# Compression stage of a hybrid decoder step: turned rows written in the order place, group, block

## The reference, cut to what matters

```python
def compress(kr, pe, w1, w2, nb):
    b, _, g, d = kr.shape                       # d = 128
    blk = kr[:, :nb * CMP_BLOCK].reshape(b, nb, CMP_BLOCK, g, d) + pe[None, None, :, None, :]
    blk = jnp.transpose(blk, (0, 1, 3, 2, 4)).reshape(b, nb, g, CMP_BLOCK * d)
    return jax.nn.silu(blk @ w1) @ w2           # w1: 4096 x 256, w2: 256 x 128
```

## Time and profile before

| | |
|---|---|
| median of 3 runs | 3240.89 us (3238.18 to 3242.6) |
| span of the profiled execution | 3241.6 us |
| PE busy | 2938.7 us, 91% of the span |
| PEld, DVE, ACT, POOL busy | 2604.9, 1365.9, 711.1, 131.9 us |
| line 1041, keys, MATMUL x512 | 118.2 us busy, 393 ns each |
| line 1041, values, MATMUL x512 | 117.2 us busy, 390 ns each |
| compress stage, keys | about 1155 to 1352 us of the span |
| compress stage, values | about 1352 to 1555 us of the span |
| granted clock over the span | 0.943 |

### The profile page before, as it was taken

How to read it: one execution, slowest core, us unless ns; L and a number is a source line. 1 busy time by engine, 2 the same in 40 slices (tenths; PEclk the granted TensorE clock), 3 DMA queues, 4 the chain that set the end, 5 groups by cost and what they waited for, 6 DMA issues and landing times. The chain is left out here.

```text
span 3241.6 us, 56390 instructions
## 1 busy us (share of the span) xinstructions
PE 2938.7 (91%) x22144; PEld 2604.9 (80%) x22144; DVE 1365.9 (42%) x2213; ACT 711.1 (22%) x1085; POOL 131.9 (4%) x150
## 2 busy tenths in 40 slices
PE   7699999999995879798889798897999999999897
PEld 3499999999993468688554465797999999999897
DVE  2422252222243547566573377435444333433434
ACT  2211222111221122121000255322222222222222
POOL 0000030000140000000000000000000000000000
PEclk8799999999996989899897799998999999999898
DMA  9666666676646643131789745432233333333421
GB/s 340 227 195 193 183 197 221 210 239 214 198 124 161 205 138 104 56 109 52 231 269 308 234 131 173 141 91 67 82 97 97 94 98 97 98 93 114 118 79 53
DMA packets 594873, 496.86 MB, mean 153 GB/s; under 512 B 37148, under 2 KB 515885, under 8 KB 593885
## 3 DMA queue, kind: packets, MB, share of 16 engines
q1 hardware_dynamic: 527912, 408.44, 42.5%
q10 hardware_dynamic: 58992, 60.59, 5.7%
q0 software_dynamic: 7840, 26.10, 2.1%
HBM read 460.02 MB, written 48.70 MB: 157 GB/s over the span
## 5 line engine op out<-in xcount | busy, mean ns | idle before, releaser
L146 PE MATMUL psum<-h_high,w_high 128*128 128x260 f32 x4992 | 1010.4, 284 | 21.6 <-DVE w_low L133 21.6
L146 PE MATMUL psum<-h_high,w_low 128*128 128x260 f32 x4992 | 1007.8, 284 | 0.0
L146 PE MATMUL psum<-h_low,w_high 128*128 128x260 f32 x4992 | 1006.2, 283 | 0.0
L146 PEld LDWEIGHTS psum<-h_high,w_high 128*128 128x128 f32 x4992 | 771.1, 189 | 35.9 <-issue 30.1
L146 PEld LDWEIGHTS psum<-h_high,w_low 128*128 128x128 f32 x4992 | 771.6, 189 | 0.0
L146 PEld LDWEIGHTS psum<-h_low,w_high 128*128 128x128 f32 x4992 | 769.5, 189 | 0.0
L133 DVE TENSOR_TENSOR w_low<-w,w_high 128x2048 fp32r<-128x2048 f32 x162 | 371.6, 2295 | 548.2 <-ACT w_high L128 548.2
L128 ACT ACTIVATE w_high<-w 128x2048 fp32r<-128x2048 f32 x162 | 309.1, 1909 | 461.3 <-PE psum L146 361.2
L628 DVE COPY pj_out<-psum 128x260 f32<-128x260 f32 x66 | 28.3, 429 | 387.4 <-PE psum L146 387.4
L576 ACT ACTIVATE pj_out<-psum 128x260 f32<-128x260 f32 x66 | 25.6, 387 | 590.3 <-PE psum L146 590.3
L199 PE MATMUL psum<-w,c 128*32 128x512 f32 x768 | 104.3, 656 | 25.6 <-DMA w<-in_w_ada 16.9
(11 more groups left out here) (357 smaller groups left out, 2729.2 us busy)
## 6 DMA issues: line engine op xcount, KB each, us to landing
w<-in_w_ada SPq DMA_DIRECT2D x96, 1024.0 KB, 7.7
w<-in_w_in_att SPq DMA_DIRECT2D x65, 1024.0 KB, 11.6
w<-in_w_in_conv SPq DMA_DIRECT2D x64, 1024.0 KB, 6.1
proj<-pj_out POOLq DMA_DIRECT2D x66, 260.0 KB, 4.7
cz_pgk<-in_cache_nsa_cmp_k SPq DMA_DIRECT2D x128, 128.0 KB, 2.2
cz_pgv<-in_cache_nsa_cmp_v SPq DMA_DIRECT2D x128, 128.0 KB, 2.1
w<-in_w_out_att SPq DMA_DIRECT2D x16, 1024.0 KB, 6.6
w<-in_w_out_conv SPq DMA_DIRECT2D x16, 1024.0 KB, 5.9
```

Source lines behind the costliest of these rows:

```text
L146: mm = pe.matmul(k.psum[:, banks + hf, 0:HC], w[:, kt, :], x[:, kt, hf * HC:(hf + 1) * HC], start=(kt == 0 and m == 0), stop=(kt == KT - 1 ...
```

## The change

`xt` holds the same numbers in the order place, group, block. The copy from PSUM (still one instruction for 512 columns of a bank) reads its bank in order and writes each number 128 columns (512 bytes) behind the one before it, 32 times, then goes on with the next block. The stationary operand of line 1041 becomes 128 adjacent columns. The prompt's rows keep their order and their strided read, under the name `xp` in the same memory. No instruction is added, removed or moved on any engine, and the tile has the same size.

```diff
@@ -994,7 +994,8 @@
         pe_t = k.sb("cz_pet" + which, [P, CB], ctx=ctx)
         pe_b = k.sb("cz_peb" + which, [P, CH], ctx=ctx)
         pg = k.sb("cz_pg" + which, [P, 2, PG // 2, 256], ctx=ctx)
-        xt = k.sb("cz_xt" + which, [P, 2, G, PAST], ctx=ctx)
+        xt = k.sb("cz_xt" + which, [P, 2, CB, G * NCB], ctx=ctx)
+        xp = xt[:, 1, :, :].rearrange("p l c -> p (l c)")[:, 0:G * T]
         x = k.sb("cz_x" + which, [P, CH], ctx=ctx)
         e = k.sb("cz_e" + which, [P, CH], ctx=ctx)
         hc = k.sb("cz_hc" + which, [P, CH], ctx=ctx)
@@ -1006,7 +1007,7 @@
                 sp.dma_start(pe_n[:, :], k.i["cmp_pe_" + which][0]).then_inc(w_got, 16)
                 sp.dma_start(w2[:, :, :], k.i["cmp_w2_" + which][0].rearrange("(c d) n -> d c n", d=P)).then_inc(w_got, 16)
                 t = KC if keys else VC
-                sp.dma_start(xt[:, 1, 0, 0:G * T].rearrange("p (g c) -> p g c", g=G), k.proj[t:t + 2, :, 0:T].rearrange("g p c -> p g c")).then_inc(prompt_in, 16)
+                sp.dma_start(xp.rearrange("p (g c) -> p g c", g=G), k.proj[t:t + 2, :, 0:T].rearrange("g p c -> p g c")).then_inc(prompt_in, 16)
                 with sp.Fori(0, NS) as s:
                     for hf in range(2):
 
@@ -1030,15 +1031,14 @@
                 pe.wait_ge(prompt_in, 16)
                 for l in range(CB):
                     a = l % 4
-                    blocks = xt[:, 1, 0, 0:G * T].rearrange("p (n l) -> p n l", l=CB)[:, :, l]
+                    blocks = xp.rearrange("p (n l) -> p n l", l=CB)[:, :, l]
                     mm = pe.matmul(ps[32 * a:32 * a + 32, 3, 0:CH], blocks, w1[:, l, :], start=(l < 4), stop=(l >= CB - 4))
                 mm.then_inc(parts, 1)
 
                 def hidden(b):
 
                     for l in range(CB):
-                        rows = xt[:, b, :, :].rearrange("p g (n l) -> p (g n) l", l=CB)[:, :, l]
-                        mm = pe.matmul(ps[:, b, 0:CH], rows, w1[:, l, :], start=(l == 0), stop=(l == CB - 1))
+                        mm = pe.matmul(ps[:, b, 0:CH], xt[:, b, l, :], w1[:, l, :], start=(l == 0), stop=(l == CB - 1))
                     mm.then_inc(hid, 1)
 
                 def second(j2, n):
@@ -1095,7 +1095,8 @@
 
                     for c in banks:
                         act.wait_ge(turned, j2 * 8 + (8 * s + c + 9))
-                        copy(xt[:, s % 2, :, c * 256:(c + 1) * 256], ps[:, 4 + c % 2, :].rearrange("p (g q) -> p g q", g=G)).then_inc(kept, 1)
+                        to = xt[:, s % 2, :, :].rearrange("p l (g n) -> p g n l", g=G)[:, :, c * 8:(c + 1) * 8, :]
+                        copy(to, ps[:, 4 + c % 2, :].rearrange("p (g n l) -> p g n l", g=G, l=CB)).then_inc(kept, 1)
 
                 def exp(j2, n):
                     act.wait_ge(x_done, j2 + (n + 1))
```

## The result

| | before | after |
|---|---|---|
| median | 3240.72 us (4 runs, 3238.18 to 3242.6) | 3269.85 us (4 runs, 3266.6 to 3281.89) |
| span of the profiled execution | 3241.6 us | 3271.3 us |
| ratio | | 1.0091, 95% interval 1.0075 to 1.0108 |

The account below looks back on a forecast made before the run. TensorE, busy 91% of the span, was taken as the bound, each round being turning then product. Copies +33.6, rounds 0 and 1 +2.9, product -9.6 gave +26.9 us on 3240.9: 3268 us, range 3230 to 3300.

Parts of the forecast that it names:

- The product: Line 1041's 64 matmuls: adjacent columns save 9.4 ns per record, 9.6 us over 16 products; bounds 0 and 9.6.
- The copy: ScalarE's copy from PSUM into `xt`: writing single numbers 512 bytes apart takes 1.03 us instead of 0.595, at half rate.
- The end from the weight loads: Copy time if ScalarE's stride costs as in TensorE's weight loads, 1.46 against 0.84 ns a column: 0.91 us.
- The end from VectorE: Copy time if ScalarE is held to VectorE's 1.75 ns a column when reading every 32nd column: 1.06 us.
- What a copy costs a round: First copy to `hct` grows from 5.01 to 7.81 us, +2.80 a round, 33.6 us in 12 rounds; ScalarE sets the pace.
- Rounds 0 and 1: First rounds of both stages, with page waits: round 1's `hct` comes 1.44 us later, twice, 2.9 us in all.
- The sum: Whole kernel: 33.6 + 2.9 - 9.6 = +26.9 us on the median 3240.9, giving 3268 us.
- the likeliest case: Whole kernel with copies at half rate: 3268 us, own range 3252 to 3282, chance 57%.
- the rival that got 12%: The granted clock falls as TensorE stands between transposes: 2.0 us a round, 24 more in 12 rounds, 3292 us; 12%.
- ScalarE writing as fast with a step as without: Rival on the copies: they stay as they were and only the product's 9.6 us gain remains, 3231 us; 15%.
- the worse price for steps of exactly 512 bytes: Rival on the copy: steps fall on the same part of memory; at a third of the rate 1.465 us, 3317 us; 10%.
- The sign that was named for it: In the profile after, the granted clock of the two stages leaves 0.95; the forecast would then be wrong.

Follow-up runs that it names:

- the product alone: Against the changed kernel, the copy writes in the old order and the product keeps 128 adjacent stationary columns: 3234.32 us, ratio 0.9965.

## Why the prediction was right, step by step

- **The product.** Forecast 0.60 us a product (9.4 ns a record), measured 0.55 and, alone, 20.45 instead of 21.0 us a round. That the stride of the stationary operand cost this, and that it would go, is shown by the product alone; 13.98 us for 64 is 216 ns from start to start, where 215 was taken from line 930. How the 309 ns load made it is not shown: the starts were 224 ns apart, less than one load's record, so the 8.6 ns do not follow from the load's length.
- **The copy.** Forecast 1.03 us by half rate, measured 1.053. That the write would cost is shown as a mechanism: it is the write, in single numbers, and neither the read nor the step of exactly 512 bytes. That the size came out is in part luck. The end from the weight loads gave 0.91, too low. The end from VectorE (1.06) rests on two rows of line 1924, with 8 and 16 columns, and the trace before has two more of them:

```profile
L1924 DVE TENSOR_TENSOR pa_lc<-psum,pa_t 128x4 f32<-128x4 f32 x8 | 1.3, 162 | 0.3
...
L1924 DVE TENSOR_TENSOR pa_lc<-psum,pa_t 128x12 f32<-128x12 f32 x8 | 1.3, 160 | 0.0
```

From 4 to 16 columns the slope is (170 - 162) / 12 = 0.67 ns a column and not 1.75, so these rows don't show half rate.
- **What a copy costs a round.** Forecast +2.80, measured +2.31 (7.32 us) and, alone, +2.34. The term mis-sized is how long a copy holds ScalarE: 0.10 less than its record was carried over from the short copy, but six in a row take 5.51 us, so from one start to the next (5.51 - 1.05) / 5 = 0.89 us, 0.16 less than the record. The exponential cost less as well (1198.83 to 1199.13, 0.30 instead of 0.37). Who waits for whom was right: ScalarE sets the pace (no gap in its six copies), and of the first 0.68 us, which were counted as waits for banks, four banks took 0.52 away.
- **Rounds 0 and 1.** Forecast 1.4 us each stage from round 1. Its `hct` for the keys came at 1181.67 instead of 1180.42, with the stage's start earlier by about 1.1 us (the first copy at 1162.22 instead of 1163.30): 2.3 us. The clock was low there in both traces, at different places (transposes of 1.97 us for 8), so this term was not separated.
- **The sum.** The spans differ by 29.7 us. Between the first and the last `hct` of the two stages, twelve full rounds without a fall of the clock give 21.6 us (turning and product together), and the shorter product gives back 1.7 in the four intervals that turn nothing. Together that is +19.9, where 33.6 - 9.6 = +24.0 was forecast. The falls of the clock cost 6.7 us after and 1.5 before, a net +5.2, where the likeliest case had nothing; this is a part of the rival that got 12%, in four rounds and not in all twelve. The remaining 4.6 us lie in the starts of the two stages and behind the second; 2.9 was forecast for rounds 0 and 1. So an error of -4 us and one of +5 stand against each other, and that the forecast came out within 2 us of the median is luck. The direction is not: the turning alone costs +2.3 us a round and the product gives back 0.55. The chances treated the likeliest case and the clock's as if only one could come, and both did in part.
- **Of the other rivals,** ScalarE writing as fast with a step as without is refuted by 1053 ns, and the worse price for steps of exactly 512 bytes did not come: 1053 ns is near half rate, and a step of 528 bytes is no faster (1101). The argument against the clock's, that the new gaps are below 1 us, was too weak: the wait for `hct` had grown from 0.74 to 1.13 us and was not priced. The sign that was named for it, a granted clock of the stages other than 0.95, came for one stage: 0.92 for the values (1363 to 1583 us after, 0.95 before), while the keys stayed at 0.96 (1155 to 1363 us) in spite of their round of 24.45 us. The falls are seen better round by round than in a stage's mean.

## What to carry to other kernels

When a layout is turned for one engine's sake, price the other side of the same tile in the same sum, and let the reorder fall on the side that takes it for nothing: here the same layout cost +29 us with the step on ScalarE's write and gained 6 us with the step on its PSUM read. A pair of adjacent numbers was enough for nearly the full rate (611 against 595 ns a copy). Before buying buffers for one engine, ask where its standing time will then lie: here 3.5 us a round with one piece of 2.48 cost more clock than 3.2 us in gaps of at most 1.13.

## What the runs showed that was not expected

- Four banks under the long copies made the kernel some 18 us slower, with the turning itself no longer, and 20 transposes whose result nobody reads took it back.
- A step of 528 bytes wrote slower than one of 512 (1101 against 1053 ns a copy), in one trace; the reason stays open.
- TensorE's transposes with an identity in another column order, and a PSUM destination in runs of 4, kept their pace (294 against 295 ns in the rows above, the second in the changed kernel).
